# Stick-breaking attention: scores divided between two row halves of the array by exchanged copies, value products between two column halves

## The reference, cut to what matters

```
z = jnp.einsum('bhqd,bhkd->bhqk', qb, kf)
mask = key_pos[None, :] < q_pos[:, None]
log_beta = jax.nn.log_sigmoid(z)
log_fail = jnp.where(mask, log_beta - z, 0.0)
after = lax.cumsum(log_fail, axis=3, reverse=True) - log_fail
w = jnp.where(mask, jnp.exp(log_beta + after), 0.0)
return jnp.einsum('bhqk,bhkd->bhqd', w, vf)
```

## Time and profile before

| | |
|---|---|
| median of 3 runs | 3150.19 us (3149.43 to 3156.2) |
| profiled execution | 3153.32 us; its span, first to last instruction, 3151.5 us |
| TensorE matmul | busy 98% of the span, 14595 records |
| VectorE, ScalarE, GpSimd | busy 43%, 19%, 65% |
| TensorE's granted clock | 0.991 of full speed in the mean |
| chain that ended last | TensorE 92%, VectorE 3%, DMA, GpSimd, ScalarE and issue 1% each |

### The profile page before, as it was taken

The page is one execution under the profiler, slowest core; times in us unless marked ns, Lnnn a source line. Parts: engine busy times, 40 slices in busy tenths (PEclk is TensorE's granted clock), DMA queues, the critical chain, the costliest instruction groups (busy, mean ns, idle before and its releaser), DMA issues.

```text
span 3151.5 us, 38636 instructions
## 1 busy us (share of the span) xinstructions
PE 3078.0 (98%) x14595; PEld 2525.4 (80%) x14595; DVE 1357.9 (43%) x1587; ACT 604.2 (19%) x993; POOL 2063.2 (65%) x1473
## 2 busy tenths in 40 slices
PE   7999989999999999999999999999999999999998
PEld 4878857788888888887888888888888878888887
DVE  3652374888435322365244332243323652433321
ACT  3362262212121000132011100111001320111100
POOL 2614386688877777644677776777776447777764
PEclk9999999999999999999999999999999999999999
DMA  5301162232332223421223323323234212232332
GB/s 200 94 28 54 60 214 67 81 97 94 90 106 93 93 86 100 127 85 54 94 96 104 93 89 92 111 91 97 86 92 132 80 62 93 93 100 96 93 90 75
DMA packets 327727, 298.17 MB, mean 95 GB/s; under 512 B 6596, under 2 KB 321988, under 8 KB 324296
## 3 DMA queue, kind: packets, MB, share of 16 engines
q1 hardware_dynamic: 324344, 290.49, 29.1%
q10 hardware_dynamic: 3280, 6.26, 0.7%
HBM read 292.53 MB, written 2.10 MB: 93 GB/s over the span
## 4 chain that ended last, share of the span: by engine, by line
PE 92%; DVE 3%; DMA 1%; POOL 1%; issue 1%; ACT 1%; SPq 0%; DVEq 0%; POOLq 0%; ACTq 0%
PE pm L1988 25%; PE pm L1990 25%; PE pm L1989 25%; PE pa L1988 2%; PE pa L1989 2%; PE pa L1990 2%; PE pm L2289 1%; POOL wlo L591 1%; PE pm L2036 1%; PE pm L2037 1%; PE pm L2038 1%; DMA modraw<-in_w_mod 1%; DMA raw<-in_w_mod 1%; PE pa L2237 1%; PE pm L2537 1%
## 5 line engine op out<-in xcount | busy, mean ns | idle before, releaser
L591 POOL TENSOR_TENSOR wlo<-raw,whi 128x512 fp32r<-128x512 f32 (+1 forms) x1096 | 1444.5, 1348 | 22.8
L587 POOL TENSOR_SCALAR whi<-raw 128x2048 fp32r<-128x2048 f32 (+1 forms) x274 | 482.5, 1761 | 987.4 <-PE pm L1990 607.4
L1988 PE MATMUL pm<-hh,whi 128*128 128x512 f32 x2392 | 939.8, 393 | 6.2 <-DVE hl L1599 3.1
L1989 PE MATMUL pm<-hl,whi 128*128 128x512 f32 x2392 | 932.7, 390 | 0.0
L1990 PE MATMUL pm<-hh,wlo 128*128 128x512 f32 x2392 | 932.6, 390 | 0.0
L1988 PEld LDWEIGHTS pm<-hh,whi 128*128 128x128 f32 x2392 | 450.0, 188 | 104.3 <-issue 6.4
L1989 PEld LDWEIGHTS pm<-hl,whi 128*128 128x128 f32 x2392 | 449.9, 188 | 94.7 <-issue 2.6
L1990 PEld LDWEIGHTS pm<-hh,wlo 128*128 128x128 f32 x2392 | 449.8, 188 | 93.7
L1988 PE MATMUL pm<-uh,whi 128*128 128x512 f32 x880 | 343.2, 390 | 0.7 <-POOL wlo L591 0.7
L1990 PE MATMUL pm<-uh,wlo 128*128 128x512 f32 x880 | 342.7, 389 | 0.0
L1989 PE MATMUL pm<-ul,whi 128*128 128x512 f32 x880 | 342.6, 389 | 0.0
(11 more groups left out here) (426 smaller groups left out, 3839.7 us busy)
## 6 DMA issues: line engine op xcount, KB each, us to landing
raw<-in_w_ffn SPq DMA_DIRECT2D x88, 1024.0 KB, 5.3
raw<-in_w_in SPq DMA_DIRECT2D x62, 1024.0 KB, 5.1
raw<-in_w_ffn SPq DMA_DIRECT2D x64, 704.0 KB, 4.5
raw<-in_w_up SPq DMA_DIRECT2D x22, 1024.0 KB, 5.0
raw<-in_w_mod SPq DMA_DIRECT2D x16, 1024.0 KB, 5.0
raw<-in_w_out SPq DMA_DIRECT2D x12, 1024.0 KB, 5.0
raw<-in_w_down SPq DMA_DIRECT2D x16, 704.0 KB, 4.5
modraw<-in_w_mod SPq DMA_DIRECT2D x8, 1024.0 KB, 15.9
```

The lines of the kernel that those rows point to most:

```text
L587: nc.gpsimd.tensor_scalar(h, r, 1.0, 1.0, ALU.mult, ALU.mult).then_inc(hi_done, 1)
L591: last = nc.gpsimd.tensor_tensor(o[:, c], r[:, c], h[:, c].bitcast(F32), ALU.subtract)
L1988: nc.tensor.matmul(out, wh, ah, start=start, stop=False)
L1989: nc.tensor.matmul(out, wh, al, start=False, stop=False)
```

## The change

The scores of blocks 1 and 2 are taken from copies of q and k in which the two partition halves are exchanged (`q_sw`, `k_sw`), so that blocks 0 and 3 use one row half of the array and blocks 1 and 2 the other, 640 columns each. The value products of blocks 1 and 2 write the other 64 partitions of the bank, so blocks 0 and 3 use one column half and blocks 1 and 2 the other, again 640 columns each. The two partial sums have then to be added: ScalarE copies the second one to `ysb_t` in the right partitions (a new counter `sb_half`), and VectorE adds it in PSUM ahead of `ysb_h`; for it ScalarE waits for the value product of each head. The copies come by four DMAs of 64 partitions on ScalarE's queue, for which the first scores wait (`halves_swapped`). They lie where `decay` was; `decay` is loaded after the last head's `sp_h`, and `mixc_loaded` is asked for nine of ten before the heads and for the tenth before the retention's products with it. `signs_made` becomes part of `mixc_made`.

```diff
+        q_sw = tile_at("q_sw", [P, 2, T], 0)
+        k_sw = tile_at("k_sw", [P, 2, T], 2)
+        ysb_t = tile_at("ysb_t", [P, 2, T], 34)
...
-                for dst, name in ((decay, "c_decay"), (rope, "c_rope"), (trineg, "c_trineg"), (onesneg, "c_onesneg"),
-                                  (dmask, "c_dmask"), (invcnt, "c_invcnt")):
+                for p, (src, dst) in enumerate(((q_sb, q_sw), (k_sb, k_sw))):
+                    act.wait_ge(pm_free[p], u0 + 1)
+                    for o in (0, 64):
+                        act.dma_start(dst[64 - o:P - o, :, :], src[o:o + 64, :, :]).then_inc(halves_swapped, 16)
+                for dst, name in ((dmask, "c_dmask"), (trineg, "c_trineg"), (onesneg, "c_onesneg"), (rope, "c_rope"), (invcnt, "c_invcnt")):
                     act.dma_start(dst[:], io[name]).then_inc(mixc_loaded, 16)
...
                     nc.scalar.activation(sp_h[:], sp_[:], ACT.Copy).then_inc(sp_high, 1)
+                    if h == SB_HEADS - 1:
+                        act.dma_start(decay[:], io["c_decay"]).then_inc(mixc_loaded, 16)
...
+                    hp, op = slice(64 * (h % 2), 64 * (h % 2) + 64), slice(64 - 64 * (h % 2), P - 64 * (h % 2))
+                    act.wait_ge(sb_out, SB_HEADS * l + h + 1)
+                    nc.scalar.activation(ysb_t[hp, h // 2, P:], pm[0][op, 0, P:], ACT.Copy).then_inc(sb_half, 1)
...
                     v.wait_ge(sb_out, SB_HEADS * l + h + 1)
+                    v.wait_ge(sb_half, SB_HEADS * l + h + 1)
+                    nc.vector.tensor_tensor(pm[0][hp, 0, P:], pm[0][hp, 0, P:], ysb_t[hp, h // 2, P:], ALU.add).then_inc(sb_hi, 1)
+                    v.wait_ge(sb_hi, 2 * (SB_HEADS * l + h) + 1)
                     nc.vector.tensor_copy(ysb_h[hp, h // 2, :], pm[0][hp, 0, :]).then_inc(sb_hi, 1)
...
+                v.wait_ge(mixc_loaded, 16 * 10 * (l + 1))
                 decayed(0)
...
-                pe.wait_ge(mixc_loaded, 16 * 10 * (l + 1))
+                pe.wait_ge(mixc_loaded, 16 * (10 * l + 9))
...
                     if h:
                         pe.wait_ge(lw_done, m)
+                    else:
+                        pe.wait_ge(halves_swapped, 16 * 4 * (l + 1))
                     for j in range(TT):
-                        nc.tensor.matmul(pa[j][:, 0:LIVE[j]], k_sb[hp, h // 2, P * j:P * j + P], q_sb[hp, h // 2, P * j:],
+                        k, q, rows = (k_sw, q_sw, op) if j in (1, 2) else (k_sb, q_sb, hp)
+                        nc.tensor.matmul(pa[j][:, 0:LIVE[j]], k[rows, h // 2, P * j:P * j + P], q[rows, h // 2, P * j:],
...
-                        last = nc.tensor.matmul(pm[0][hp, 0, P * j:], v_sb[:, j, 64 * h:64 * h + 64], w_[:, LIVE_AT[j]:LIVE_AT[j] + LIVE[j]],
-                                                start=j == 0, stop=j == TT - 1)
+                        last = nc.tensor.matmul(pm[0][op if j in (1, 2) else hp, 0, P * j:], v_sb[:, j, 64 * h:64 * h + 64], w_[:, LIVE_AT[j]:LIVE_AT[j] + LIVE[j]],
+                                                start=j < 2, stop=j >= 2)
```

More of the change, by code:

```diff
@@ L327, in build @@
         sb_hi = sem("sb_hi")
-        signs_made, sp_high, sp_low, z_taken, lw_done = sem("signs_made"), sem("sp_high"), sem("sp_low"), sem("z_taken"), sem("lw_done")
+        sp_high, sp_low, z_taken, lw_done = sem("sp_high"), sem("sp_low"), sem("z_taken"), sem("lw_done")
+        halves_swapped, sb_half = sem("halves_swapped"), sem("sb_half")
         win_done, pd_done, pool_out, pool_scaled, pool_hi, pool_done = (
@@ L1155, in mix @@
                 nc.scalar.activation(mrcol[:], pa[1][:, 0:TT], ACT.Copy).then_inc(rcol_done, 1)
-                for dst, name in ((decay, "c_decay"), (rope, "c_rope"), (trineg, "c_trineg"), (onesneg, "c_onesneg"),
-                                  (dmask, "c_dmask"), (invcnt, "c_invcnt")):
+                for p, (src, dst) in enumerate(((q_sb, q_sw), (k_sb, k_sw))):
[3 more added lines that the diff above has]
+                for dst, name in ((dmask, "c_dmask"), (trineg, "c_trineg"), (onesneg, "c_onesneg"), (rope, "c_rope"), (invcnt, "c_invcnt")):
                     act.dma_start(dst[:], io[name]).then_inc(mixc_loaded, 16)
-                act.wait_ge(mixc_made, 3 * l + 1)
+                act.wait_ge(mixc_made, 5 * l + 1)
                 for g in range(4):
@@ L1781, in fill @@
                     if i == 7:
-                        v.wait_ge(mixc_made, 3 * l + 3)
+                        v.wait_ge(mixc_made, 5 * l + 3)
                     dst = {3: rraw[0][:], 4: rraw[1][:], 7: u[:, :, PAD:], 8: sil[0][:], 9: sil[1][:], 10: gates[:, 0], 11: gates[:, 1], 12: gates[:, 2]}[i]
@@ L1840, in sb_heads_out @@
                     v.wait_ge(sb_out, SB_HEADS * l + h + 1)
+                    v.wait_ge(sb_half, SB_HEADS * l + h + 1)
+                    nc.vector.tensor_tensor(pm[0][hp, 0, P:], pm[0][hp, 0, P:], ysb_t[hp, h // 2, P:], ALU.add).then_inc(sb_hi, 1)
+                    v.wait_ge(sb_hi, 2 * (SB_HEADS * l + h) + 1)
                     nc.vector.tensor_copy(ysb_h[hp, h // 2, :], pm[0][hp, 0, :]).then_inc(sb_hi, 1)
-                    v.wait_ge(sb_hi, SB_HEADS * l + h + 1)
+                    v.wait_ge(sb_hi, 2 * (SB_HEADS * l + h) + 2)
                     nc.vector.tensor_tensor(ysb_l[hp, h // 2, :], pm[0][hp, 0, :], ysb_h[hp, h // 2, :].bitcast(F32), ALU.subtract).then_inc(pm_free[0], 1)
[L1845 to L1848, removed]
+                v.wait_ge(mixc_loaded, 16 * (10 * l + 9))
+                v.wait_ge(mixc_made, 5 * l + 3)
+                nc.vector.tensor_copy(trineg_r[:], trineg[:]).then_inc(mixc_made, 1)
+                nc.vector.tensor_copy(onesneg_r[:], onesneg[:]).then_inc(mixc_made, 1)
                 for h in range(SB_HEADS):
@@ L2508, in mix @@
                 for h in range(SB_HEADS):
-                    hp = slice(64 * (h % 2), 64 * (h % 2) + 64)
+                    hp, op = slice(64 * (h % 2), 64 * (h % 2) + 64), slice(64 - 64 * (h % 2), P - 64 * (h % 2))
                     m = TT * (SB_HEADS * l + h)
@@ L2519, in mix @@
                         if n_ == 0:
-                            pe.wait_ge(signs_made, 2 * (l + 1))
+                            pe.wait_ge(mixc_made, 5 * (l + 1))
                             pe.wait_ge(sp_high, SB_HEADS * l + h + 1)
```

## The result

The changed kernel took 3168.78 us (median of four runs, 3167.57 to 3172.72) beside 3151.51 for the kernel before on the same chip (four runs, 3149.43 to 3156.2). The ratio is 1.0058, interval 1.0045 to 1.0071: slower by some 17 us, where no change was forecast. Its profiled execution has a span of 3165.8 us, 14.3 more than before's. The other 3 us lie in which executions were profiled: the changed kernel's (3167.57) is the lowest of its four, before's (3153.32) is above its median. What follows explains the 14.3.

A forecast was written before the change was run, and what follows sets the result against it. TensorE, busy 98% of the span, was taken as the bound. Per layer -0.93 + 1.4 - 2.13 + 0.9 + 0.77 = 0.0, put on the earlier runs' median: 3150 us, range 3136 to 3156.

The forecast's parts named there:

- head 0: First head of the attention: slab ends 1.07 us earlier, 0.14 lost to a new wait, 0.93 us saved.
- head 1: Second head: VectorE's rotation meets GpSimd, TensorE's wait grows from 1.2 to 5 us, 1.4 us lost.
- head 2: Third head: shorter values and scores save 2.13 us, VectorE's chain being ready 0.4 us before the slab's end.
- head 3: Last head: GpSimd stops VectorE's long windows, the slab behind the sums starts late, 0.9 us lost instead of 2.14 won.
- the mechanism: VectorE and GpSimd in the heads: exclude each other for whole instructions; a 0.30 us mask takes 1.4 beside a subtraction.
- The fourth step: VectorE's rotation in head 1: fourth of six operations waits for GpSimd's multiplication, to 1360.3, and ends at 1360.85, taking 2.3 us.
- The tail: After the last value product: ScalarE's new copy precedes the two pt copies, so the retention starts 0.77 us later.
- a wait ahead of the first scores: Slower rival: loads behind the four copies come late, TensorE waits 1 to 4 us per layer, 3152 to 3158; chance 0.08.
- The early mask: Rival in the heads: first mask starts before GpSimd's subtraction, each chain 1.2 us earlier, 3137 us; chance 0.2.
- All 17 us arrive: Rival for both layers: VectorE's chain never binds and the whole halving saving shows, 3133 us; chance 0.05.
- In between: Rival: one of the two stalls, in head 1 or head 3, misses GpSimd, 3142 to 3146 us; chance 0.08.
- Columns don't overlap: Rival at the value products: the column halves don't run at once, values stay 2.30 us, 3155 us; chance 0.05.

The follow-up runs named there:

- experiment 2: Changed kernel with the second half of VectorE's first rotation behind head 1's addition and the long windows one head earlier: 3146.54 us, ratio 0.9982.
- 10: Changed kernel without VectorE's addition of the two partial sums, so the output lacks key blocks 1 and 2: 3159.72 us, ratio 1.0019.
- experiment 3: Changed kernel with the two scaled copies of the pooled sums ahead of the last head's partial-sum copy on ScalarE: 3166.96 us, ratio 1.0044.
- Experiment 4: Changed kernel with constants and pool weights ahead of the exchange copies, rotation half and long windows moved, pooled copies ahead of the last partial-sum copy: 3136.47 us, ratio 0.9948.
- 8: Kernel before, nothing halved, with five extra VectorE copies ahead of the release of head 1's slab: 3163.93 us, ratio 1.0035.
- experiment 9: Kernel before, nothing halved, with two extra VectorE copies ahead of the release of head 1's slab: 3158.36 us, ratio 1.0016.
- experiment 1: Changed kernel with ScalarE issuing constants and the four pool weights ahead of the four exchange copies: 3161.98 us, ratio 1.0027.

## Why the prediction was wrong, and where it was right

Head by head it was right. The sums of the steps for head 0 in layer 1, head 1, head 2 and head 3 are within 0.15 us of the trace, as the table shows, and the mechanism is the one named. VectorE after, in head 1, against the earlier trace rows:

```profile
1355.42 0.55 DVE L1854 TENSOR_TENSOR pm<-pm,ysb_t 64x384 f32<-64x384 f32 x1
...
1360.04 0.69 DVE L1810 TENSOR_TENSOR q_r<-rt,rt 128x512 f32<-128x512 f32 x1
1360.76 2.28 DVE L1807 TENSOR_TENSOR rt<-rraw,rope 128x512 f32<-128x512 f32 x1
1362.97 1.75 DVE L1808 TENSOR_TENSOR rt<-rswap,rope 128x512 f32<-128x512 f32 x1
1364.75 1.63 DVE L1810 TENSOR_TENSOR q_r<-rt,rt 128x512 f32<-128x512 f32 x1
1366.30 1.21 DVE L1791 TENSOR_TENSOR v_r<-pm,mrcol 128x1024 f32<-128x1024 f32 x1
```

GpSimd, against the earlier trace rows:

```profile
1360.49 2.02 POOL L591 TENSOR_SCALAR whi<-raw 128x2048 fp32r<-128x2048 f32 x1 [7.01 <-issue]
1362.59 6.15 POOL L595 TENSOR_TENSOR wlo<-raw,whi 128x512 fp32r<-128x512 f32 x4
```

The fourth step (0.69 where nothing stops it) starts 0.27 behind L591 and takes 2.28, the fifth and sixth 1.75 and 1.63 beside the subtractions, as the prediction had them; the addition is 0.55. TensorE's slab then starts at

```profile
1367.66 0.55 PE L2052 MATMUL pm<-whi,hh 128*128 128x256 f32 x1 [4.63 <-DVE v_r L1791]
```

Experiments 2 and 10 confirm this chain. In head 3 GpSimd's multiplication and subtraction stopped L1834 and L1837 (1.76 and 1.38 us, the latter 0.43 in the earlier trace rows), which are L1822 and L1825 of before, the steps that the prediction named, and the slab started after 2.94 us of waiting for "3 us".

The tail: 0.97 lost for 0.77. ScalarE after:

```profile
1444.18 0.48 ACT L1209 ACTIVATE ysb_t<-pm 64x384 f32<-64x384 f32 x1 [13.46 <-PE pm L2556]
1444.68 1.26 ACT L1213 ACTIVATE pt<-pa,col 128x512 f32<-128x512 f32 x2
```

From the start of ScalarE's copy to the start of the retention the prediction had 1.73 us (1437.77 to 1439.50), the trace has 1.91. It took off 0.1 us for an overlap of the copy with the first of the two behind it, and the records show none; TensorE then follows ScalarE's end by 0.15 us, not 0.1. The mechanism holds, and experiment 3 takes 2.04 us away with its cause.

**What failed, first: "a wait ahead of the first scores", the slower rival, had 0.08 and 0 in the sum.** It counted 13 issues of ScalarE's queue, gave the last load the landing of the trace before (2.3 to 3.4 us) and found it 0.3 us under the limit. The whole stage stands 0.55 us later in this trace. That taken off, the thirteen issues ended 0.9 us later than it said (8.7 us of issuing in place of 7.8), the last packet came 5.0 us behind their end in place of 3.4, and the scores started another 0.5 us behind that packet, which was not counted. With the margin of 0.3 taken off, that makes the 2.6 us. The largest part is the landing: the step took it as a property of the load. Before, the loads were through when SyncE's 1 MB set in; moved back by the four copies they landed beside it. With +2.6 and +2.4 us this rival came true in addition to the forecast, not in its place: both together give 3155 on the prediction's own terms, inside its range.

**Second, and the larger part: the price of a wait.** Each step counted a wait of TensorE at its length. The clock that TensorE comes back with was in no term, although the forecast itself named waits of 5 and 3 us where the kernel before had none over 1.6 in its mixers. It started from TensorE "at the full granted clock in all 40 slices", but a 9 in that row is any mean of 90% or more over 79 us, and the kernel before has eight falls under such digits. Of the 13.6 us in the two layers some 8.5 are work at half clock; experiments 2 and 4 (the halves stay, the waits go, the clock stays full where they were) and 8 (the wait alone, no halves) show the cause. A forecast that had taken it in could have given bounds, but not said which of the shorter waits would be followed by a fall (last section).

**The rivals.** *The early mask* is not it: head 1's first mask is stopped by the subtraction that started 0.15 us ahead of it, and takes 1.29 us; undisturbed it is 0.30.

```profile
1348.26 1.29 POOL L595 TENSOR_TENSOR wlo<-raw,whi 128x512 fp32r<-128x512 f32 x1
1348.41 1.29 DVE L1868 COPY_PREDICATED pa<-dmask,lowest 128x128 f32<-128x128 uint32 x1 [1.06 <-PE pa L2534]
```

Each product in full fp32 runs as two passes, one record each. In head 0 the second pass of block 1 starts at 1320.20, 0.10 us before that of block 0, and is the shorter one; yet no release of z_ready comes when it is through (1320.68 by the trace's modelled ends). The first comes at 1320.90, when block 0 is (1320.89), the second at 1320.94. So completions are counted in program order. The rule of the Trainium skill that the prediction cited (TensorE: Matmul & The Clock Gate, Part 3, The mechanism: matmuls start and end in program order) agrees with this trace for the ends. For the starts it does not: block 1's second pass stands behind block 0's in the program and started ahead of it. *All 17 us arrive* (3133) is not what this kernel did, since VectorE's chain binds in heads 1 and 3. Experiment 4, in which it never binds, comes near it with 3136.5: of its 19.3 us in the two stages 16.5 are the halving's and 2.8 the order's. *In between* is out too: both stalls met GpSimd. *Columns don't overlap* is refuted by values at 1.23 us.

## What to carry to other kernels

When an engine is given less work, price the waits that open behind it with the clock it will have afterwards, and hand the saved time to the chain that becomes late: here a few instructions put elsewhere in VectorE's and ScalarE's order turned 0.6% slower into 0.5% faster. Two edits that are each neutral can lose together (here 0.9996, 0.9994 and 1.0058), where a chain of short operations of one engine lies just ahead of a long operation of another; ask how many of them fall behind its start. When small loads are queued behind new transfers, ask what they will land beside, and issue early whatever needs nothing from the stage.

## What the runs showed of the hardware

A wait of TensorE of 2.8 us was followed by half clock in one layer and not in the other (experiment 9), with the same instructions around it. In the stages of all these traces and their tails, each of the eleven waits from 3.2 to 5.0 us was followed by a fall. Of those from 1.97 to 2.95 us some were and some were not: in the changed kernel 2.94 and 2.36 were, 2.55, 2.87 and twice 1.97 were not; in experiment 1 the 1.97 us of the tail were, in both layers; in experiment 2 the 2.95 us for the pool weights were not. None followed a wait of 1.7 us or less. The falls lasted about 3.4 or 6.8 us, and one of them cost 1.4 to 2.9 us of TensorE's time. What decides in the middle range stays open.

Small loads beside a large one: four loads of 16 KB, in packets of 256 B, landed a median of 3.4 us after their issue in the kernel before and 2.5 in experiment 1, where no weight load ran beside them, and 5.1 (the last 5.6) beside a 1 MB load in packets of 1 KB on another queue, which itself took 5.3 us in place of 3.6. Loads that set in with the large one or up to 2.3 us behind it landed with its last packet. No run changed the packets' size.
